# Weight buffers at another start address in a split-precision transformer kernel

## The reference, cut to what matters

```python
h = x @ w_in                                  # even mixer: 1024 -> 3584, then retention and stick-breaking
m = y @ w_out
x = layer_norm(ALPHA * x + m, ...)
h = x @ w_up                                  # 1024 -> 5632, causal convolution of width 3 over positions
f = (silu(g) * u) @ w_down                    # 2816 -> 1024
# second block: the same with differential attention
# third block: hybrid mixer (state space scan + windowed attention), cross attention, gated FFN
```

## Time and profile before

| | |
|---|---|
| median of 3 runs | 2815.21 us (2813.67 to 2837.34) |
| profiled execution | 2830.1 us, span of its trace 2828.4 us |
| mean granted TensorE clock in it | 0.984 |
| PE busy | 2655.8 us, 94% of the span |
| PEld busy | 2438.5 us, 86% |
| DVE, ACT busy | 1453.1 us (51%), 1245.2 us (44%) |
| weight units loaded | 405 of 512 KB, 3.3 us from issue to landing (median) |

### The profile page before, as it was taken

How to read it: one execution, slowest core, us unless ns; L and a number is a source line. 1 busy time by engine, 2 the same in 40 slices (tenths; PEclk the granted TensorE clock), 3 DMA queues, 4 the chain that set the end, 5 groups by cost and what they waited for, 6 DMA issues and landing times.

```text
span 2828.4 us, 52418 instructions
## 1 busy us (share of the span) xinstructions
PE 2655.8 (94%) x20916; PEld 2438.5 (86%) x20916; DVE 1453.1 (51%) x2514; ACT 1245.2 (44%) x2045; POOL 83.8 (3%) x157
## 2 busy tenths in 40 slices
PE   7998999999998699999989988889988998999998
PEld 7985899999996399999978776679966996899998
DVE  3233476553425766554467877762376344433333
ACT  3335354332425644432365777852465234333321
POOL 0000000000000000000001211200000000000000
PEclk9998999999999999999999999999999999999999
DMA  6420122223321022223353454532211231222232
GB/s 181 122 67 0 43 89 93 93 97 101 112 97 53 1 75 97 96 89 116 101 187 124 164 201 156 178 130 93 89 51 53 94 108 45 75 97 96 96 105 68
DMA packets 74693, 278.20 MB, mean 98 GB/s; under 512 B 9642, under 2 KB 9674, under 8 KB 74048
## 3 DMA queue, kind: packets, MB, share of 16 engines
q1 hardware_dynamic: 60816, 217.42, 22.9%
q0 software_dynamic: 13744, 58.88, 6.8%
HBM read 267.03 MB, written 9.24 MB: 98 GB/s over the span
## 4 chain that ended last, share of the span: by engine, by line
PE 78%; DVE 9%; ACT 5%; issue 4%; DMA 4%; DVEq 0%; ACTq 0%; POOL 0%; POOLq 0%; SPq 0%
PE acc L338 65%; PE acc L369 2%; DMA res_tmp<-scratch_rows 2%; PE ps L813 1%; DMA w_raw<-in_stream 1%; PE ps L369 1%; ACT w_hi L313 1%; DVE big L1602 1%; DVE w_lo L319 1%; PE ps L453 1%; DVE big L1276 1%; DVE big L2178 1%; PE acc L1467 1%; PE ps L802 1%; PE ps L1745 1%
## 5 line engine op out<-in xcount | busy, mean ns | idle before, releaser
L338 PE MATMUL acc<-x_split,w_hi 128*128 128x256 f32 x7968 | 1258.6, 280 | 17.7 <-DVE x_split L1363 12.0
L338 PEld LDWEIGHTS acc<-x_split,w_hi 128*128 128x128 f32 x7968 | 1076.0, 190 | 22.3 <-issue 16.2
L319 DVE TENSOR_TENSOR w_lo<-w_raw,w_hi 128x1024 fp32r<-128x1024 f32 x405 | 493.0, 1221 | 608.2 <-ACT w_hi L313 608.2
L338 PE MATMUL acc<-x_split,w_lo 128*128 128x256 f32 x3984 | 789.7, 280 | 0.0
L313 ACT ACTIVATE w_hi<-w_raw 128x1024 fp32r<-128x1024 f32 x405 | 424.8, 1054 | 578.6 <-PE acc L338 527.4
L338 PEld LDWEIGHTS acc<-x_split,w_lo 128*128 128x128 f32 x3984 | 610.0, 190 | 0.0
L338 PE MATMUL acc<-big_r,w_hi 128*128 128x256 f32 x3560 | 559.1, 279 | 7.7 <-DVE big_r L2231 3.4
L338 PEld LDWEIGHTS acc<-big_r,w_hi 128*128 128x128 f32 x3560 | 478.1, 189 | 9.8 <-issue 3.6
L338 PE MATMUL acc<-big_r,w_lo 128*128 128x256 f32 x1780 | 351.8, 279 | 0.0
L338 PEld LDWEIGHTS acc<-big_r,w_lo 128*128 128x128 f32 x1780 | 270.9, 189 | 0.0
L1847 ACT ACTIVATE res_tmp<-res_tmp 128x512 f32<-128x512 f32 (+3 forms) x256 | 121.1, 551 | 46.9 <-DVE res_tmp L1872 45.8
(11 more groups left out here) (291 smaller groups left out, 2583.3 us busy)
## 6 DMA issues: line engine op xcount, KB each, us to landing
w_raw<-in_stream SPq DMA_DIRECT2D x405, 512.0 KB, 3.3
res_tmp<-scratch_rows POOLq DMA_DIRECT2D x128, 320.0 KB, 6.0
scratch_bias<-res_tmp POOLq DMA_DIRECT2D x1, 2560.0 KB, 55.0
res_tmp<-in_x SPq DMA_DIRECT2D x2, 1024.0 KB, 7.7
res_tmp<-scratch_bias POOLq DMA_DIRECT2D x8, 256.0 KB, 4.4
scratch_x<-res_tmp POOLq DMA_DIRECT2D x1, 2048.0 KB, 9.0
scratch_kv<-big POOLq DMA_DIRECT2D x1, 2048.0 KB, 9.5
res_tmp<-scratch_x POOLq DMA_DIRECT2D x1, 2048.0 KB, 8.6
```

Source lines behind the costliest of these rows:

```text
L319: dve.tensor_tensor(w_lo[:, u.slot], w_raw[:, u.slot], w_hi[:, u.slot].bitcast(F32), ALU.subtract).then_inc(lo_done, 1)
L338: mm = pe.matmul(a[:, h], w, AR[:, x + k, h], start=(k == 0 and w is wh and x == hi and h.start == 0), stop=(k == total - 1 and w is wl), ...
```

## The change

The placeholder gets another size; nothing else is edited.

```diff
         base = (nc.sbuf_base + 63) // 64 * 64
-        ctx.enter_context(nc.sbuf_tensor("arena_room", [P, N_SLOTS * S + 16], F32))
+        ctx.enter_context(nc.sbuf_tensor("arena_room", [P, N_SLOTS * S + (base - nc.sbuf_base) // 4], F32))
```

## The result

| | before | after |
|---|---|---|
| median | 2826.28 us (2813.67 to 2846.16, 4 runs) | 2877.66 us (2876.23 to 2880.86, 4 runs) |
| profiled execution, span | 2830.1, 2828.4 us | 2876.75, 2875.1 us |
| ratio after / before | | 1.0168, 95% interval 1.0118 to 1.0217 |

The change makes the kernel 1.7% slower: outside the range of 2803 to 2838, and on the side that had a chance of 7%. The spans differ by 46.7 us.

The account below looks back on a forecast made before the run. PE's own matmul pace, 113 or 118 ns, was taken to bound the kernel. All terms were 0, so 2830.1 + 0 = 2830.1 us for the profiled execution and 2815 us for the median, range 2803 to 2838.

Parts of the forecast that it names:

- (a): PE's reads of `w_hi` and `w_lo` at L338, L369, L1467: taken as 0, bounded by 37 us gained and 46 lost.
- a third pace: Sign that the forecast is wrong: matmuls at a pace other than the expected 113 and 118 ns.
- the loss of one of the two: Sign that the forecast is wrong: the 113 or the 118 ns pace vanishes from the long stretches.
- The bad end of (a): PE's weight reads: at most 10,500 matmuls go from the short to the long pace, 4.4 ns each, 46 us lost.
- Rival A: Relative start of weights and operands chooses PE's pace: -37 or +46 us; over 1%: 5% faster, 4% slower.
- Nothing measurable: Rival D, the forecast itself: whole kernel stays within 1%, at 2815 us, one or two stretches perhaps changing pace; chance 88%.
- (b): ACT's copy and DVE's subtraction, 405 each: at most 6 us per engine, nearly all hidden by waits; taken as 0.
- (c): Transfers into `w_raw`, `par` and `const`: a 32-byte start might add 6 to 37 us; taken as 0.
- (d): `par`, `const` and `small` as operands: columns already read at every multiple of 4 bytes, so 0.
- B: Weight loads before L338's matmuls: rows straddling 64-byte pieces cost 12.5 ns each, hidden, or 235 us uncovered (3050); chance 2%.
- C: Kernel's start: transfers at a 32-byte start are slower, +6 to +37 us; chance of over 1%: 1%.
- The note on the spread: Profiled execution, 14.9 us above the runs' median: one long stretch in the other pace gives 14 or 12.5 us.

Follow-up runs that it names:

- on_grid: Against the kernel before, weight buffers, `par`, `const` and `small` moved to start exactly on the operands' grid (offset 0): 2907.6 us, ratio 1.0327.
- all_up_32: Against the kernel before, arena and weights both moved 32 bytes up, keeping the 64 bytes between them: 2804.53 us, ratio 0.9982.
- hi_lo_stay: Against the kernel before, `w_raw` moved to offset 0 and `par`, `const`, `small` to 256, `w_hi` and `w_lo` staying at 64: 2826.48 us, ratio 0.9993.
- operands_up_32: Against the kernel before, only the arena moved 32 bytes up, leaving 32 bytes between weights and operands' grid: 2880.65 us, ratio 1.0237.
- lo_at_256: Against the kernel before, `w_lo` and what follows it moved to offset 256 from the operands' grid, the rest staying at 64: 2866.36 us, ratio 1.0147.

## Why the prediction was wrong

**The step that failed is (a)**, PE's reads of the weights, which I took as 0 because "both paces occur at the same addresses, so the address is not what chooses". The observation was right and the conclusion was not. That something else chooses between two paces at one distance does not say that the same two paces are on offer at every distance. At distance 64 the paces are 113.3 or 117.8 ns, at 32 they are 118.3 or 120.0, at 0 it is 120.0 alone. The prediction had named "a third pace" and the loss of one of the two as signs that it was wrong, and both came.

**The bad end of (a) came close in part by luck.** It took 10,500 matmuls from the short pace to the long one, at 4.4 ns each: 46 us, 2830.1 + 46 = 2876 on the profiled execution, and it is 2876.75. The two traces have 18,768 weight loads at L338, L369 and L1467 each; taken in sixes, 8,136 were at the short pace, and they lost 42.7 us, 5.2 ns each, since the new paces are above the long one. Another 9,960 at the long pace lost 9.4 us, for which the bound had nothing, and groups with waits in them gave 5.4 back. (18,800 was right; L338 alone has 17,292 of them, 83% of all matmuls and not 81%.) Rival A, in its slower form, had the place right, and the idea that the relative start of weights and operands matters. It still had one of the two old paces chosen, where new ones came. Its "full price", 46 us on top of 2815, is near the 51 us between the medians; I gave it 4%. Its argument against, "the weights still miss the grid by 32 bytes", assumed that being on the grid would be good: `on_grid` is the worst, with 120.0 ns throughout.

**That the change does less than it says**, 32 bytes and not 64, is right and was read from the addresses, but "Nothing measurable, since the change moves 32 bytes and reaches no grid" was wrong. The 32 bytes it does move take the weights from the best distance tried at this width to a bad one.

**(b), (c) and (d) were right**: 1,221, 1,054 and 190 ns unchanged, landing in 3.3 us, 27.44 us in place of 27.08 on the chain for the queue at the start. `all_up_32`, with all of these buffers at an odd start, is at 0.9982, which bounds the three terms together, and `hi_lo_stay` at 0.9993 shows that their distance costs nothing either. **Rivals B and C** fell by the same `all_up_32`: the weights and the targets of the loads are off a multiple of 64 and it costs nothing.

**The note on the spread** fits. The kernel before, at distance 64, spread over 2797.5 to 2832.36 us in 13 runs of one set and 2809.57 to 2846.25 in 22 of another. The traces at distances 64 and 320 have other long pieces at other paces each time: the 2,844 matmuls that took 117.8 ns before take 113.4 in `all_up_32` (311.73 us for 2,748). Of the 18,768, the short pace holds 7,476 in `hi_lo_stay`, 8,136 in before, 11,772 at distance 320 and 15,666 in `all_up_32`, and their profiled executions took 2834.1, 2830.1, 2824.68 and 2805.57 us, in the same order. At distance 0 the four runs lie within 3.3 us, and at 32 within 4.6 (the change) and 8.0 (`operands_up_32`). That a choice of paces also spreads the runs of one kernel is not shown, as each has one trace.

**On the rule about two read ports.** The Trainium skill ("TensorE: Matmul & The Clock Gate", Step-by-step: what each phase is for) has the weight load and the moving operand read by independent ports that take no bandwidth from each other. By it (a) would have been 0. The runs do not agree: both moved together by 32 bytes cost nothing (0.9982), and moving either alone costs 1.7 to 2.4%. The measurement decides: at full clock the pace depends on where the two reads lie to each other, which two reads without any effect on each other would not show.

**What stays open.** That the cause is the two reads meeting in one part of the memory is inferred from the distance mattering, from its period of 256 bytes, from the part that the length of the matmul plays, and from the missing effect at half clock. It was not seen by itself, and no run tells a collision of the reads from another effect of the two addresses. The shape of the pattern is not explained, nor which interruption leads to which pace, nor why `lo_at_256` has 117.8 ns. Distances that are no multiple of 32 bytes were not tried, nor was the 1/16 above the columns taken apart.

## What to carry to other kernels

Where PE bounds a kernel, divide a long uninterrupted piece of the chain by its matmuls and compare the stretches with each other: values that differ at the same granted clock are a cost that no wait, share or mean length shows. Where it pays, as the 3.3% here, treat the offset between the stationary and the moving buffers as a size to be tuned on the chip like any other (here it repeated after 256 bytes), again after each change of the matmul's width; an allocation that was padded for another reason may be carrying it. When a pace comes in two values at one setting, do not conclude that the setting has no part in it, and put the end where all of it goes bad into the range.

## What the runs showed of the hardware that I had not expected

- Time against distance at 256 columns, each ratio against before in its own set: 0: 1.0327, 32: 1.0168, 64: 1 (before), 96: 1.0202, 128: 1.0173, 192: 1.0128, 256: 1.0253, 320: 0.9988. At most 6.7 ns of a matmul's 120, and 3.3% of the kernel.
- No long stretch beat 113.3 ns per 256 columns at full clock, at any distance and either width, though the columns alone make 106.7. At half clock the columns alone explain all (213.3 ns at distances 0, 32 and 64).
- 512 columns per weight load bring nothing by themselves: 1.0067 at distance 64. With the distance set to 0 they hold every long stretch at 113.3 ns per 256 columns and give the lowest ratio measured, ahead of before and of the change: 2800.85 us, 0.9904 (0.9874 to 0.9935) of the kernel before, and with the weights at 256 the same, 0.9899 (0.9858 to 0.9940).
- As means of long pieces the paces come back to the tenth of a nanosecond, in pieces of hundreds of microseconds and in different runs: 117.8, 118.3, 118.7 and 120.0 are distinct values, not noise.
